# Moving the buffers of a three-block transformer kernel to other addresses in on-chip memory

## What is computed

```python
for layer in range(2):                       # first two blocks, d_ff = 2816
    x = x + 0.5 * swiglu(rms_norm(x, g1), w_gate, w_up, w_down)
    x = x + (pool_mla_mixer if layer == 0 else gated_conv_mixer)(rms_norm(x, gm), ...)
    x = x + 0.5 * swiglu(rms_norm(x, g2), w_gate2, w_up2, w_down2)
# third block, d_ff = 2752: the same frame with a Fourier and grouped-attention mixer
x = x + 0.5 * swiglu(...); x = x + mixer(...); x = x + 0.5 * swiglu(...); x = rms_norm(x, final)
# swiglu(h) = (silu(h @ w_gate) * (h @ w_up)) @ w_down
```

## Time and profile before

| | |
|---|---|
| median of 3 runs | 2809.52 us (2809.3 to 2811.19) |
| the profiled execution's own time | 2811.45 us |
| its span in the trace | 2809.6 us |
| PE busy | 2766.3 us, 98% of the span |
| mean granted TensorE clock | 0.997 |

### The profile page before, as it was taken

How to read it: one execution, slowest core, us unless ns; L and a number is a source line. 1 busy time by engine, 2 the same in 40 slices (tenths; PEclk the granted TensorE clock), 3 DMA queues, 4 the chain that set the end, 5 groups by cost and what they waited for, 6 DMA issues and landing times.

```text
span 2809.6 us, 31389 instructions
## 1 busy us (share of the span) xinstructions
PE 2766.3 (98%) x12580; PEld 2261.5 (80%) x12580; DVE 1331.8 (47%) x1895; ACT 908.2 (32%) x1286; POOL 130.3 (5%) x130
## 2 busy tenths in 40 slices
PE   8999999999999999999999999999999999999998
PEld 6888878888888888888888888888877877788776
DVE  5444358654443444434654444344443557544432
ACT  4222226542322223222233232223222346432221
POOL 0000005300000000000000000000000114000000
PEclk9999999999999999999999999999999999999999
DMA  4332232033323333333333333333322320233322
GB/s 152 99 98 91 91 86 77 24 89 103 95 92 96 96 98 90 101 96 96 98 90 98 98 90 98 92 95 91 105 85 89 92 81 23 61 103 100 90 84 70
DMA packets 282704, 253.30 MB, mean 90 GB/s; under 512 B 8384, under 2 KB 278848, under 8 KB 282560
## 3 DMA queue, kind: packets, MB, share of 16 engines
q1 hardware_dynamic: 282560, 251.30, 29.9%
HBM read 249.17 MB, written 2.10 MB: 89 GB/s over the span
## 4 chain that ended last, share of the span: by engine, by line
PE 82%; issue 13%; DVE 3%; ACT 2%; DMA 0%; SPq 0%; POOLq 0%; POOL 0%; DVEq 0%
PE bank L380 27%; PE bank L381 27%; PE bank L382 27%; PE bank L469 1%; DVE a_mx L1235 0%; PE bank L433 0%; PE bank L422 0%; DMA raw<-in_ffn_w_gate 0%; DVE wl L1126 0%; ACT Xh L804 0%; DVE a_nb L1142 0%; ACT wh L773 0%; DVE a_KT L1138 0%; ACT a_P L857 0%; DVE X L1135 0%
## 5 line engine op out<-in xcount | busy, mean ns | idle before, releaser
L1126 DVE TENSOR_TENSOR wl<-raw,wh 128x1024 fp32r<-128x1024 f32 (+6 forms) x498 | 573.9, 1166 | 976.2 <-ACT wh L773 975.3
L380 PE MATMUL bank<-Xh,wl 128*128 128x512 f32 x2544 | 997.6, 392 | 12.9 <-DVE wl L1126 10.6
L382 PE MATMUL bank<-Xh,wh 128*128 128x512 f32 x2544 | 992.0, 390 | 0.0
L381 PE MATMUL bank<-Xl,wh 128*128 128x512 f32 x2544 | 991.5, 390 | 0.0
L773 ACT ACTIVATE wh<-raw 128x1024 fp32r<-128x1024 f32 (+6 forms) x498 | 494.9, 1009 | 1001.3 <-PE bank L382 994.9
L380 PEld LDWEIGHTS bank<-Xh,wl 128*128 128x128 f32 x2544 | 476.3, 187 | 117.0 <-issue 12.6
L381 PEld LDWEIGHTS bank<-Xl,wh 128*128 128x128 f32 x2544 | 476.4, 187 | 102.9 <-issue 1.9
L382 PEld LDWEIGHTS bank<-Xh,wh 128*128 128x128 f32 x2544 | 476.1, 187 | 103.0
L380 PE MATMUL bank<-Hh,wl 128*128 128x512 f32 x1056 | 419.0, 397 | 0.0
L382 PE MATMUL bank<-Hh,wh 128*128 128x512 f32 x1056 | 417.0, 395 | 0.0
L381 PE MATMUL bank<-Hl,wh 128*128 128x512 f32 x1056 | 417.0, 395 | 0.0
(11 more groups left out here) (264 smaller groups left out, 1583.5 us busy)
## 6 DMA issues: line engine op xcount, KB each, us to landing
raw<-in_ffn_w_gate SPq DMA_DIRECT2D x128, 512.0 KB, 3.8
raw<-in_ffn_w_up SPq DMA_DIRECT2D x128, 512.0 KB, 3.9
raw<-in_ffn_w_down SPq DMA_DIRECT2D x114, 512.0 KB, 3.5
raw<-in_c_w_in SPq DMA_DIRECT2D x24, 512.0 KB, 3.7
raw<-in_w_in SPq DMA_DIRECT2D x10, 512.0 KB, 3.8
raw<-in_a_w_in SPq DMA_DIRECT2D x8, 512.0 KB, 3.8
raw<-in_a_w_out SPq DMA_DIRECT2D x8, 512.0 KB, 3.5
raw<-in_c_w_out SPq DMA_DIRECT2D x8, 512.0 KB, 3.5
```

The costliest lines, as they stand in the source:

```text
L380: e.matmul(o, ll, rh, start=start, stop=False)
L381: e.matmul(o, lh, rl, start=False, stop=False)
L382: i = e.matmul(o, lh, rh, start=False, stop=stop)
L1126: e.tensor_tensor(lo, src, hi.bitcast(F), ALU.subtract).then_inc(wlo.up(("w", n)), 1)
```

## The change

Every buffer now begins on a multiple of 64 bytes instead of 32, and five calls ask for 2048. The order changes: `wh` moves ahead of `raw`, and the 4-byte `spare` moves from behind `par` to between `raw` and `wl`.

```diff
+    _at = -(-_at // 16) * 16 if _n >= 64 else _at
     COLS[_name] = (_at, _at + _n)
...
-        def sb(name, shape, dt):
-
-            at = -(-place[0] // 32) * 32
+        def sb(name, shape, dt, line=64):
+
+
+            at = -(-place[0] // line) * line
...
-        X = sb("X", [128, KT, T], F)
-        Xh = sb("Xh", [128, KT, T], R)
+        X = sb("X", [128, KT, T], F, 2048)
+        Xh = sb("Xh", [128, KT, T], R, 2048)
         Xl = sb("Xl", [128, KT, T], R)
+        wh = [sb(f"wh{i}", [128, CAP], R, 2048) for i in range(N_RAW)]
         raw = [sb(f"raw{i}", [128, CAP], F) for i in range(N_RAW)]
-        wh = [sb(f"wh{i}", [128, CAP], R) for i in range(N_RAW)]
+        spare = sb("spare", [128, 1], F)
         wl = [sb(f"wl{i}", [128, CAP], R) for i in range(N_RAW)]
         par = sb("par", [128, NCOLS], F)
-        spare = sb("spare", [128, 1], F)
...
-    par = np.empty((128, NCOLS), np.float32)
+    par = np.zeros((128, NCOLS), np.float32)
...
-    nc = _bacc.Bacc("TRN2", target_bir_lowering=False, num_devices=1)
+    nc = _bacc.Bacc("TRN2", target_bir_lowering=False, num_devices=1, dynamic_dma_scratch_size=1024)
```

## The result

The changed kernel takes 2831.78 us (median of 4 runs, 2831.04 to 2833.4) against 2809.9 of the kernel before (4 runs): ratio 1.0078, 95% interval 1.0061 to 1.0096. It is slower, by 22 us, where 24 us of gain were forecast. Rival (b), whose price was 2833, comes nearest to it.

A forecast was written before the change was run, and what follows sets the result against it. PE's matmul pitches were taken to bound the kernel. Gains of 21.2 (H), 1.3 (c_Y) and 1.2 us (mixers) sum to 23.7, taking 2809.5 to 2786 us, 0.84% faster; range 2705 to 2809.

The forecast's parts named there:

- Rival (b): wl's new place costs if stationary and moving operands must keep their distance modulo 512: 2833 us, chance 0.14.
- PE's pitch is the time: Whole kernel: PE busy 98% of the span, so time is the sum of matmul pitches; the rest is hidden.
- What sets Xh apart from Hh is that it lies on a multiple of 64: Matmuls of 512 columns: an operand off 64 costs 6.7 ns, whichever it is; two cost no more.
- The scores of the earlier trace as the test of it: First mixer's scores, both operands 32 past 64: three pitches in 0.70 us, 233 ns, read as supporting the address reading.
- H from 233.3 to 226.6 ns: Hidden tiles moved to multiples of 64: 3168 matmuls gain 6.7 ns each, -21.2 us.
- c_Y and the mixers' tiles: Convolution's 192 matmuls gain 1.3 us; mixers' at most 284 matmuls gain 1.2 us, of 1.9 possible.
- X from 128 to 0 past 2048: 0: New start of X, Xh, Xl and wh: no effect taken; gain bounded at 101 us from X.
- Rival (a): Round starts help X as well: one more step of 16 cycles gives 2712 us, floor 2640; chance 0.30.
- wl from 0 to 64: 0 taken: wl's less round start: no cost taken, since wl is not off 64; loss bounded at 4.2 ns on every matmul.
- The 3.1 ns at which it was to decide: Rise of the triple's mean on X from which a loss by wl's new place would decide (23.7 / 7632).
- ACT, DVE, DMA, scratch, par: nothing: Other engines, transfers, smaller scratch space and wider par: effects hidden or not counted; 3 us if ACT's cover went.

The follow-up runs named there:

- 64-alone run: The kernel before with one edit, 64 in place of 32 in the allocator: 2789.11 us, ratio 0.9923 to the kernel before.
- spare-back run: The changed kernel with the 4-byte spare put back behind par, so wl begins at a multiple of 2048: 2788.13 us, ratio 0.992 to the kernel before.

## Why the prediction was wrong

*PE's pitch is the time.* Right. In the changed kernel and in all eleven others the time lies within 5 us of what the triples of X, H and c_Y give; in the changed kernel no wait took the place of anything.

*What sets Xh apart from Hh is that it lies on a multiple of 64.* This is the step that failed. The matmuls of the earlier trace rows were two classes that differed in two ways at once: on or off 64, and at distance 0 or not from the other operand. I chose the first; the run with everything at 32 and the run with both weights at 64 show the second, modulo 256: X's triple takes 680.3 ns with every operand off 64, and 700.0 with X at 0 past 2048 and both weights at 64. Before, Hh lay 1824 beyond the weights, 32 modulo 256; the 64 was an accident of it.

*The scores of the earlier trace rows as the test of it.* There both operands were off 64 at distance 0, and 233 ns seemed to decide for the 64. With the spare put back, the same scores have both operands on multiples of 2048, still at distance 0, and take 0.69 us for three:

```profile
463.27 0.39 PE L382 MATMUL bank<-a_KT,a_QT 96*128 96x512 f32 x1
463.50 0.40 PE L383 MATMUL bank<-a_KT,a_QT 96*128 96x512 f32 x1
463.73 0.39 PE L384 MATMUL bank<-a_KT,a_QT 96*128 96x512 f32 x1
463.96 0.22 PE L514 MATMUL bank<-maskR,identR 128*128 128x128 f32 x1
```

In all thirteen traces these scores lie at distance 0 and their three pitches take 692 to 704 ns, 703 in the changed kernel, where both operands are on multiples of 2048. So this row is slow on 64 and off it, and could not test the reading. A likely reason stands in the Fourier sequence of the kernel with the spare put back, where the operands of the earlier trace rows now lie at distance 0. A new run of matmuls begins, after a first pitch of 0.31 us, with 0.23 and 0.24, and settles at 226.7 ns after about six; three matmuls end before that.

```profile
2258.38 0.47 PE L382 MATMUL bank<-wh,g_ABl 128*128 128x512 f32 x1 [1.88 <-ACT g_ABh L806]
2258.69 0.39 PE L383 MATMUL bank<-wl,g_ABh 128*128 128x512 f32 x1
2258.92 0.40 PE L384 MATMUL bank<-wh,g_ABh 128*128 128x512 f32 x1
2259.16 0.39 PE L382 MATMUL bank<-wh,g_ABl 128*128 128x512 f32 x1
...
2260.07 0.39 PE L383 MATMUL bank<-wl,g_ABh 128*128 128x512 f32 x1
2260.30 0.39 PE L384 MATMUL bank<-wh,g_ABh 128*128 128x512 f32 x1
2260.53 0.39 PE L382 MATMUL bank<-wh,g_ABl 128*128 128x512 f32 x1
2260.75 0.39 PE L383 MATMUL bank<-wl,g_ABh 128*128 128x512 f32 x1
```

X's matmuls in the kernel before, at distance 0 as well, do the same after a start-to-start gap of 0.91 us: a first pitch of 306 ns, nine of 224 to 236, and then 227. But no wait stands ahead of the scores, so for them this stays an inference.

*H from 233.3 to 226.6 ns.* Right in size, on the condition that the weights share the new address modulo 256: 680.1 or 680.2 against 700.0 a triple in the five kernels that fulfil it. In the changed kernel wh did and wl didn't, and a third of the gain was left, 6.9 us of 21.2. c_Y and the mixers' tiles fell short too: 0.4 us for 1.3, and 0.5 for 1.2 on all other matmuls together.

*X from 128 to 0 past 2048: 0.* Right; both starts give 680 when the weights go along. Rival (a) is out too: no distance and no start that was tried gave less than 680.

*wl from 0 to 64: 0 taken.* Wrong, and worth +31 us on X. The nearest row was the earlier trace rows, and it was set aside for its narrow weights. Its slices, at 128 + 640k, lie alternately 0 and 128 from Xh modulo 256, and its 230.8 lies between the 226.7 and 232.4 that the table has for these, as far as its narrow weights allow the comparison. Rival (b) had the mechanism, with 512 for 256. The 3.1 ns at which it was to decide are one matmul's share, 9.3 for a triple; X's triple rose by 12.8. That its price was close was luck: 230.8 happens to be near the 231.1 that the changed kernel has in all stages.

*ACT, DVE, DMA, scratch, par: nothing.* Consistent with the 64-alone run, which lacks the scratch and par edits and equals the spare-back run within 1 us, inside both intervals.

With nothing but the relative place of the two operands changed, the triple goes from 680 to 703 ns. The Trainium skill, "SBUF — State Buffer", section Specifications (TRN2), gives memory lines of 16 bytes; these are no explanation either, since all starts of these operands are multiples of 32. The Trainium skill, "SBUF — State Buffer", section Who interferes with whom, lists PE's read port for the moving operand and that for weight loads as independent. The pitch here does depend on how the two addresses lie to each other, and the measurement decides. What inside the chip makes the period of 256 bytes stays open, and so does the way in which neighbours of unlike distance add up.

The best version found is the changed kernel with the spare behind `par`, or, with one edited number, the kernel before with 64 in the allocator: 0.8% faster than before and 1.5% faster than the changed kernel.

## What to carry to other kernels

When a stream of matmuls has two pitches, tabulate the start of both operands, their difference included, and look for a pair of rows that agree in the one and differ in the other before choosing; a run of three matmuls is no such row, for the pitch here needed six to ten to settle. For matmuls of 512 columns, keep stationary and moving float32r buffers at the same address modulo 256 bytes, every part of a split number included. At 256 columns no loss was seen: the earlier trace rows lie at distance 0 with 120 ns, at 224 with 119. A buffer of 4 bytes put among large ones moves all that follow it: print the addresses of a layout and compare them.

## What had not been expected

A matmul's pitch depends on where its operands lie relative to each other: 226.7 ns at equal addresses modulo 256, up to 234.3 elsewhere (at 160), for 512 columns of float32r at a granted clock of 1.00. At distance 0, absolute alignment at multiples of 32, 64, 128 or 2048 showed no effect of its own. One misplaced operand slows more than the matmul that uses it: with wl 64 bytes off all three pitches of the triple rise, with wl 128 bytes off two of them. And a run of matmuls begins slower than it goes on, by up to 9 ns a pitch after the first, in the sequence shown.
